# A Trainium2 decoder-layer kernel: the MLP's first matrix product by seven block products, with operands formed by the norm

## What is computed

```python
h = layer_norm(ALPHA * x + mix, ln1_g, ln1_b)
f = jnp.einsum('btf,fd->btd', jnp.square(jax.nn.relu(jnp.einsum('btd,df->btf', h, w_mlp1))), w_mlp2)
y = layer_norm(ALPHA * h + f, ln2_g, ln2_b)
```

## Time and profile before

| what | us |
|---|---|
| median of 3 runs (lowest, highest) | 2871.43 (2864.63, 2872.89) |
| the profiled execution's own time | 2851.42 |
| its span | 2849.7 |
| end of the output projection to the first matmul of the MLP | 1243 to 1266 |
| MLP, first part | 1266 to 2073 |
| MLP, second part | 2073 to 2806 |
| second norm and output | 2806 to 2849.7 |

### The profile page before, as it was taken

The page is one execution under the profiler, slowest core; times in us unless marked ns, Lnnn a source line. Parts: engine busy times, 40 slices in busy tenths (PEclk is TensorE's granted clock), DMA queues, the critical chain, the costliest instruction groups (busy, mean ns, idle before and its releaser), DMA issues.

```text
span 2849.7 us, 52194 instructions
## 1 busy us (share of the span) xinstructions
PE 2704.9 (95%) x20801; PEld 2573.5 (90%) x20801; DVE 1612.8 (57%) x2496; ACT 890.3 (31%) x1102; POOL 52.1 (2%) x106
## 2 busy tenths in 40 slices
PE   8999999997888889989999999999979999999997
PEld 8999999985555579969999999999979999999995
DVE  5778722237753343364344344334468888888897
ACT  3111111126754441153233322222223333333334
POOL 0000000000000100000000000000000000000000
PEclk9999999998998889989999999999999999999998
DMA  8766543324034534324554544555575566655632
GB/s 249 230 226 224 152 86 85 79 73 169 0 141 171 222 116 132 122 59 132 175 172 164 170 154 158 175 175 170 184 247 177 179 195 196 193 173 182 191 110 76
DMA packets 466354, 447.92 MB, mean 157 GB/s; under 512 B 45436, under 2 KB 416340, under 8 KB 455478
## 3 DMA queue, kind: packets, MB, share of 16 engines
q1 hardware_dynamic: 461018, 379.57, 42.7%
q0 software_dynamic: 4608, 67.11, 6.2%
q10 hardware_dynamic: 652, 0.18, 0.0%
HBM read 362.98 MB, written 92.09 MB: 160 GB/s over the span
## 4 chain that ended last, share of the span: by engine, by line
PE 66%; DVE 4%; DMA 4%; issue 2%; ACT 1%; SPq 0%; DVEq 0%; POOL 0%; POOLq 0%; ACTq 0%
PE ps L1753 35%; PE ps L2099 23%; DMA sg<-in_cache_slc,idx 3%; PE ps L1897 1%; PE ps L2008 1%; PE ps L1907 1%; PE ps L1960 1%; PE ps L1973 1%; DVE pS L1330 1%; PE ps L1986 1%; PE ps L1921 1%; DVE h_t L1505 1%; DMA f_b<-f_scratch 1%; DVE h_t L1495 1%; ACT pS L804 0%
## 5 line engine op out<-in xcount | busy, mean ns | idle before, releaser
L2099 PE MATMUL ps<-f_b,w_sh 128*128 128x288 f32 x3584 | 714.7, 296 | 16.2 <-DVE h_t L1602 14.3
L2099 PEld LDWEIGHTS ps<-f_b,w_sh 128*128 128x128 f32 x3584 | 575.2, 189 | 18.7 <-DVE h_t L1602 11.5
L2099 PE MATMUL ps<-f_b,w_sl 128*128 128x288 f32 x1792 | 527.4, 294 | 0.0
L1753 PE MATMUL ps<-h_hi,w_hi 128*128 128x288 f32 x2048 | 433.3, 293 | 6.4 <-DVE h_lo L1511 6.3
L708 ACT ACTIVATE w_hi<-w_raw 128x2048 fp32r<-128x2048 f32 x125 | 239.3, 1914 | 638.9 <-PE ps L1753 634.3
L1753 PE MATMUL ps<-h_lo,w_hi 128*128 128x288 f32 x2048 | 432.0, 292 | 0.0
L1753 PE MATMUL ps<-h_hi,w_lo 128*128 128x288 f32 x2048 | 432.0, 292 | 0.0
L961 ACT ACTIVATE w_sh<-w_s 128x1024 fp32r<-128x1024 f32 (+1 forms) x256 | 237.3, 950 | 495.3 <-PE ps L2099 291.9
L2099 PEld LDWEIGHTS ps<-f_b,w_sl 128*128 128x128 f32 x1792 | 339.3, 189 | 0.0
L1753 PEld LDWEIGHTS ps<-h_hi,w_hi 128*128 128x128 f32 x2048 | 326.3, 188 | 9.0 <-DVE h_lo L1511 5.0
L713 DVE TENSOR_TENSOR w_lo<-w_raw,w_hi 128x2048 fp32r<-128x2048 f32 x125 | 286.2, 2290 | 72.9 <-ACT w_hi L708 71.2
(11 more groups left out here) (264 smaller groups left out, 2677.4 us busy)
## 6 DMA issues: line engine op xcount, KB each, us to landing
w_raw<-in_w_mlp SPq DMA_DIRECT2D x128, 512.0 KB, 4.8
w_s<-in_w_mlp SPq DMA_DIRECT2D x256, 256.0 KB, 3.9
f_scratch<-f_st SPq DMA_DIRECT2D x32, 2016.0 KB, 8.5
f_b<-f_scratch SPq DMA_DIRECT2D x56, 1152.0 KB, 8.1
w_raw<-in_w_in SPq DMA_DIRECT2D x90, 512.0 KB, 5.1
x_r<-x_scratch SPq DMA_DIRECT2D x16, 576.0 KB, 5.1
wb<-in_cache_win SPq DMA_DIRECT2D x8, 1024.0 KB, 9.7
w_raw<-in_w_out SPq DMA_DIRECT2D x64, 128.0 KB, 2.9
```

Of the source, the lines that this page charges most:

```text
L1753: last = nc.tensor.matmul(out[:, h, :], w[:, k * P:(k + 1) * P], x[:, k, h * TH:(h + 1) * TH], start=(k == 0 and m == 0), stop=(k == KT - ...
L2099: last = nc.tensor.matmul(ps[:, bank, 0:TH], w[b][:, at_, cols], f[:, k, x, :], start=(start and k == 0 and n == 0), stop=(k == CK - 1 and ...
```

## The change

The first part of the MLP is made of seven block products as well. What it does, place by place:

- **Norm.** Behind the norm's scale and shift, for each pair of h tiles (8 pairs, `j`), DVE forms four sums and differences of the quadrants (`h_sums`), ACT writes the high parts of seven operands (`h_high`) and DVE the low parts (`h_low`), into `h_b`. h itself is stored to HBM by SP (`y_scratch`, 8 DMAs) and loaded again, in 8 DMAs, in the second part's first 8 steps (`y_load`), where `take` multiplies it by ALPHA.
- **First part.** It has 64 units of 7 products x 12 matmuls, two units (the two halves of the contraction, `h`) for each pair of column blocks `i`: 5,376 matmuls. The weight operands of a unit are made as those of a step in the second part, by the same seven DVE instructions and four ACT instructions (`unit_act`, `first_half`, `second_half`). The products add up over the two units in seven PSUM banks; ACT and DVE then combine them to the four quadrants (`keep_1`, seven `up` additions on DVE), ACT takes relu and square of all four at once (`relu_square`, 128 x 1152 each), and DVE and ACT form `f_st` as before (`f_sums`, `f_high`, `f_low`).
- **Loads.** The weights of a unit come as four blocks of 256 KB (`w_blocks`), after `low_22` of the unit two before. `f_store(i)` stands between the loads of units 2i+4 and 2i+5.

The core of the diff:

```diff
-            w1_pair(0)
-            w1_pair(1)
-            with sp.Fori(2, KP) as i:
-                w1_pair(i)
-                f_store(i - 2)
...
+            def up_load(q, h):
+
+                sp.wait_ge(z_l[M4], 2 * q + h - 1)
+                w_blocks(w1_v, h, q, h)
...
+            for j in range(MP):
+                sp.wait_ge(l_aff, 2 * j + 2)
+                sp.dma_start(y_dram[:, 2 * j:2 * j + 2, :], h_t[:, 2 * j:2 * j + 2, :]).then_inc(y_sv[j // 3 if j < 3 else 1], 16)
+            up_load(1, 0)
+            up_load(1, 1)
+            with sp.Fori(0, KP - 2) as i:
+                up_load(i + 2, 0)
+                f_store(i)
+                up_load(i + 2, 1)
...
+            def first_half(i):
+
+
+                t, n = 2 * i, 64 * i + 64
+                close_7(i - 1)
+                low_12(t, 0)
+                dve.wait_ge(z_l[M3], t + 1)
+                sum_1(t + 1, 1, n)
+                sum_23(t + 1, 1)
+                close_4(i - 1)
+                low_22(t, 0)
+                low_14(t + 1, 1)
+                sum_4(t + 1, 1)
+                low_56(t + 1)
+                f_sums(i - 1)
+
+            def second_half(i, before=True):
+
+
+                t, n = 2 * i + 1, 64 * i + 64
+                low_12(t, 1)
+                dve.wait_ge(z_l[M3], t + 1)
+                sum_1(t + 1, 0, n + 64)
+                sum_23(t + 1, 0)
+                if before:
+                    f_low(i - 1)
+                low_22(t, 1)
+                low_14(t + 1, 0)
...
+            def h_sums(j):
...
+                nc.vector.tensor_tensor(raw[:, 0:3:2, :], view[:, 0:1, :].broadcast_to([P, 2, TH]), view[:, 1:3, :], ALU.subtract).then_inc(h_t3, 1)
+                dve.wait_ge(h_t3, 3 * j + 1)
+                nc.vector.tensor_tensor(raw[:, 1, :], view[:, 2, :], raw[:, 0, :], ALU.subtract).then_inc(h_t3, 1)
+                dve.wait_ge(h_t3, 3 * j + 2)
+                nc.vector.tensor_tensor(raw[:, 3, :], view[:, 3, :], raw[:, 1, :], ALU.subtract).then_inc(h_t3, 1)
```

More of the change, by code:

```diff
@@ L76 @@
 NSTEP = NCH * MP
+NU = 2 * KP
 WC = CK * P
@@ L914, in _ @@
[L914 to L944, removed]
@@ new lines, in _, with unit_act @@
+            for k in range(4):
+                shift(k)
+            for j in range(MP):
+                h_high(j)
+                if j < MP - 2:
+                    shift(2 * j + 4)
+                    shift(2 * j + 5)
+                if j == 6:
+                    act.wait_ge(z_p[M5], 1)
+                    high_14(1, 1, 64)
+            act.wait_ge(z_p[M3], 1)
+            high_56(1)
+            act.wait_ge(z_p[M7], 1)
+            high_12(1, 1)
+            def unit_act(t, u, n, middle=None):
@@ L989, in step_act @@
                 high_14(t + 1, 1 - u, n + 64 * u)
+                if middle is not None:
+                    middle()
                 act.wait_ge(z_p[M3], t + 1)
@@ new lines, in _ @@
+            norm_dve(0, h_t)
+            dve.wait_ge(l_sd, 2)
+            for k in range(4):
+                scale_1(k)
+            for j in range(MP):
+                h_sums(j)
+                if j < MP - 2:
+                    scale_1(2 * j + 4)
+                    scale_1(2 * j + 5)
+                h_low(j)
+                if j == 5:
+                    dve.wait_ge(z_l[M3], 1)
+                    sum_1(1, 1, 64)
+                    sum_23(1, 1)
+                if j == 6:
+                    low_14(1, 1)
+                    sum_4(1, 1)
@@ L1684, in _ @@
-            square(0, KP - 1)
-            sum_1(0, 0, 64)
-            sum_23(0, 0)
-            low_14(0, 0)
-            sum_4(0, 0)
-            low_56(0)
-            dve.wait_ge(f_y, KT)
-            chunk_dve(0, first=True)
-            with dve.Fori(1, NCH - 1) as c:
+                        step_dve(r + MP - 2 + u, u, n + 32 * MP - 64, MP - 2 + u, before=MP - 3 + u, sums=sums, last=u == 1)
+            for q in range(MP):
+                dve.wait_ge(y_rd[q % 4], 16 * (q // 4 + 1))
+                step_dve(q, q % 2, 32 * (NU + q - q % 2) + 64, q, before=q - 1 if q else None, fresh=True, fresh_before=True, opening=q == 0)
+                if q == 0:
+                    f_sums(KP - 1)
+                if q == 1:
+                    f_low(KP - 1)
@@ L1754, in gemm @@
                                                     start=(k == 0 and m == 0), stop=(k == KT - 1 and m == 2))
-                    if free is not None and k in (3, 7, 11):
-                        last.then_inc(free, 1)
                 last.then_inc(s_gemm, 1)
@@ new lines, in _, with down_product @@
+            pe.sem_inc(z_p[M4], 1)
+            for h in range(2):
+                up_half(0, h, first=True)
+            with pe.Fori(1, KP) as i:
+                for h in range(2):
+                    up_half(i, h)
+            pe.wait_ge(z_l[M4], NU)
+            up_product(M4, 1)
+            def down_product(m, u, p, start=False):
+                bank = DOWN_B if m in (M3, M5) else DOWN_C if m == M2 else DOWN_A[u]
+                f = f_b[m][p if m != M4 else 0]
+                product(m, bank, lambda k, x: f[:, k, x, :], start, True, adds=not start)
```

560 lines of the change are left out of this document (335 added, 225 removed).

## The result

The changed kernel takes 2887.78 us (median of 9 runs, 2878.87 to 2890.86), the kernel before in 9 runs 2864.63 (2848.25 to 2872.89): ratio 1.0079, 95% interval 1.0055 to 1.0103. It is slower by 0.8%, 23 us. The direction was forecast; the size was forecast at 44 us, and the absolute time at 2915.

The account below looks back on a forecast made before the run. PE was taken to bound the first part, and after the change a loop of DVE, store and load. First part 39 us later plus opening 5 gave 44, on the median 2871.4: 2915 us, range 2860 to 2962.

Parts of the forecast that it names:

- What waits: First part's loop: sum_1 of each odd unit waits for its four blocks behind the store; DVE waits 4 us a pair.
- The loop, 25.6 us a pair: First part: 14.0 us of DVE, 0.04 to the store's issue, 11.5 to the blocks' landing; PE needs 22.2.
- the recorded lower bound of 10.4 us: From the store's issue to the odd unit's last block: at least 10.4 us, taken as 11.5, at most 12.6.
- the last M4: End of the first part: product M4 of the last unit adds 1.6 us to the sum of 789.5.
- The norm, first pair: From the norm's scale to the first pair's end: 47 us of operands plus 12 of products, 59 us, ending at 1322.5.
- The opening and the end: Second part's opening: operand loads, y_loads and stores cost 25 us for 20, 5 later (0 to 12); the end unchanged.
- against the median 2871.4 + 44: Last step of the sum: the 44 us added to the earlier kernel's median of 2871.4, giving 2915 us.
- PE's term: First part: 5,376 matmuls at 132 ns take 710 us in place of 797, 87 us less if PE never waits.
- The queue hides the load: Rival, first part's loop: blocks land within 8 us of the store's issue, a pair takes 22.2, total 2816; chance 0.15.
- the rule behind it: Skill's rule: one queue's descriptors start in order but are pipelined, reads and writes in separate queues; blocks near 6.3 us.
- the clock drops in the pauses: Rival, first part: PE's pauses lower its clock, 2 us more a pair, total 2975; chance 0.08 with anything longer.
- DVE by itself: Rival, first part: DVE's own work bounds a pair, 19.2 us plus waits, less than 22.2, so changes nothing; no chance given.

Follow-up runs that it names:

- five operands ahead: Changed kernel with the store cut in two: five of its seven operands stored ahead of the odd unit's blocks, two behind them; 2844.88 us in one execution.
- the repaired loop: Changed kernel with the loop's store of a pair issued behind the odd unit's four blocks instead of ahead of them; 2795.71 us (4 runs), ratio to before 0.9761.

## Why the prediction was right or wrong

**What waits.** Right, and shown by the moved store: the odd unit's blocks behind `f_store`, 4.0 us ahead of `sum_1` once a pair, none for the even units.

**The loop, 25.6 us a pair.** Measured 25.35. The DVE stretch was right to the digit (14.00). From the end of `f_low` to the next late `sum_1` it is 0.17 + 11.17 = 11.34 us, not 0.04 + 11.5, because behind the store alone the last block takes 3.5 us more, not 4.0. (With the recorded lower bound of 10.4 us the loop's range begins at 24.4, not at 24.9, and its upper bound of 12.6 is not worked out from a row; the measured value lies inside either way.) Over 29 pairs, and with the 1.6 us for the last M4 that did not show, this is 10 us of the 15 that the sum was too high against the profiled execution.

**The norm, first pair.** From the first scale to the end of the pair 59.5 us, forecast 59. Its end came at 1318.0 and not at 1322.5 because the out-projection had ended at 1237 in place of 1243, 6 us earlier, and the stretch from there to the end of the pair was 1.4 us longer than forecast. Both profiles of the changed kernel show 1237, the nine other kernels with the same code up to there 1238 to 1248, and the kernel before 1243 and 1244; it varies from execution to execution, and by what stays open.

**The opening and the end.** 5 forecast, 4.8 measured (4.3 in the second part, 0.5 behind it). The second loading of h is 1.9 of it. Of the opening's whole 23 us I had put everything on transfers; the long third step goes with `f_high` and `f_low` of the last pair. That the term came out right is in part luck.

Against the profiled execution the sum is corrected by the loop (-10.4), the out-projection's early end (-5.9), the norm (+1.4) and the rest (-0.3): 44 - 15.2 = 28.8 us, the difference of the own times (2880.25 - 2851.42).

**The step that failed: "and against the median 2871.4 + 44".** The profiled execution stood 20 us below the median, as the table said, and I carried the difference over as if the 20 us lay in stages that both kernels share. The second profile, of an execution at 2877.65 us, shows them in the very stage that the change replaces: a pair took 192 x 130.0 ns = 24.96 us in the first profile and 25.6 in the second, so that PE's term is 87 us in one and about 107 in the other. At the slower pace the same sum gives 44 - 20 = 24 us. The second miss is the loop's term ("29 at 25.6", and 1.6 for the last M4), 10 us too high by the landing. The two together bring 2915 to 2885, against 2887.78 measured; the out-projection's early end falls away here, since the profiled execution of the changed kernel lay 7.5 us below its own median. Between second profiles the two kernels differ by 4 us, between first ones by 29; the medians lie between, at 23.

The mechanism of the loop was right; what failed is the price of PE's work before, read from an execution that was not typical. The kernel before was timed 33 times in four sets: 7 executions took 2847 to 2857 us (4 of 9, 2 of 10, none of 7, 1 of 7), 26 took 2865 to 2878, and none lay between. Two of its executions were profiled, one at each pace. That every time of the lower group is one at the faster pace is therefore argued, and what sets the pace is open. A sign of it stood in the first trace: its out-projection, with the same matmuls, ran at 133 ns, and its first part at 130.

**The rivals.** "The queue hides the load" and the rule behind it did not hold with the store ahead, whatever the queue. That the clock drops in the pauses did happen, at no price. These are stretches of 2 us around a pause (columns as in rows 1):

```profile
1398.00:1400.00 2.00, 0.04 (x1) 0.00 (x0) 2.00 (x4) 1.40 (x3) 0.00 (x0) 1.00 0.00 0
1400.00:1402.00 2.00, 1.67 (x10) 1.67 (x11) 0.97 (x2) 1.84 (x2) 0.00 (x0) 0.79 0.72 212
1402.00:1404.00 2.00, 2.00 (x10) 2.00 (x10) 1.81 (x2) 1.11 (x2) 0.00 (x0) 0.50 1.05 296
1404.00:1406.00 2.00, 2.00 (x15) 2.00 (x14) 1.93 (x4) 0.82 (x1) 0.00 (x0) 0.86 0.06 17
1406.00:1408.00 2.00, 2.00 (x17) 2.00 (x17) 1.97 (x4) 2.00 (x3) 0.00 (x0) 1.00 0.00 0
```

After 2 us in which PE ran next to nothing the granted clock went from 2.4 GHz to half of it (1.2 GHz, 0.50) for 3 to 4 us and came back. It did so in 12 of 28 pairs (0.93 in each of these, 0.97 over the 29; 1.00 with the shorter pauses of five operands ahead), and the loop was still 25.35, since DVE and the DMAs set it and PE needs 22.2 of it. PE stood still for 59 of 734 us, 2.0 us a pair, not the 3 forecast. DVE by itself was no bound either: in the repaired loop it was busy for 178 of 200 us, and PE never waited.

## What to carry to other kernels

Where a store and a load share a turn of a loop and the load is wanted sooner, issue the load first: here the blocks were wanted 8 us later, the store a whole pair later, and the order alone cost 91 us; giving the store to another engine's queue at the same time did not replace the order. Add up the closed loop of waits (engine stretch, issue, landing) from rows, and find the landing up to which it is hidden, before pricing the engine whose work the change saves. And when the profiled execution is not at the median, ask in which stage the rest lies: if it may lie in the one that is replaced, it belongs to the term's range. A second profile, or another stage with the same instructions, can tell.

## What had not been expected of the hardware

- The same plain matmul stream ran at 130.0 ns a matmul in one execution and at 133.3 in another, both with granted clock 1.00 and no wait, while the out-projection kept to 133 in both and the streams of block products to 132.2 in every one.
- A store issued by ACT and loads issued by SP 0.6 us later were moved and landed in the order of their issue (1.97 MB of the store against 0.01 MB of the loads in the first 5.7 us), to 0.1 us as from one queue.
- POOL's subtractions beside DVE's made each DVE instruction with two SBUF inputs 0.6 us or more longer (1.05 to 1.65, 1.35 to 1.95 us).
